# Order of the row stores, throwaway products on TensorE, and the order behind the experts in a hybrid decoder step

## Chip, cores and metric

One NeuronCore of a Trainium2 chip runs the whole program; the kernel is written by hand in Bass, with its own semaphores. The metric is the device time of one execution in microseconds. The kernel before took 856.63 us, the median of three runs (854.76 to 859.32).

## What is computed

A decoder layer over 520 rows of width 1024: 512 prompt rows and 8 sample rows. A mixer (gated short convolution beside four-head retention) is followed by a mixture of 32 experts and a gated embedding. Cut from the reference to what the change touches:

```python
h = h + mixer(rmsnorm(h, g_mix), ...)
x = rmsnorm(h, g_ffn)
# top-1 of 4 groups, then top-2 of its 8 experts; cw holds the two weights of a row
for e in range(32):
    hid = silu(x @ w_gate[e]) * (x @ w_up[e])       # width 512
    y = y + cw[:, e:e+1] * (hid @ w_down[e])
h = h + y
gate = sigmoid(rmsnorm(h, g_ple) @ w_ple_gate)      # 1024 x 1024
h = h + (p @ w_ple_proj) * gate                     # p: 256 columns
y_out = rmsnorm(h, g_final)
```

All weights are f32; those of the experts are 201 MB, and each expert is read once.

## The kernel before

**Head (0 to 277 us).** The rows lie transposed in SBUF. TensorE (PE) runs a list of jobs, `JOBS`; each writes one of four pairs of PSUM banks, and ScalarE (ACT) or VectorE (DVE) reads it. The last jobs are `wo` (output projection, eight column blocks), `tp` (transposing the new rows back, eight blocks), `lg` (router logits) and `ss` (sums of squares), then routing: DVE scales the logits by 1/rms (`route_logits`), picks group and experts (`route_choose`), and PE runs `rk` (ranks of each row in its expert, from `chosen`), `ix` and `iy` (the index tables of 64 places for each expert, from the masks of `hot_rows`) and `tot` (rows per expert). `ix` becomes `index`, which the gathers use.

**Rows in DRAM.** The experts gather their rows from `h_rows` in DRAM, half a row of 512 columns and 16 columns of 1/rms at a time. POOL (GpSimd) writes it: `store_rows` for each of the four entries of `STORES`, each one large store (prompt rows) and one small (sample rows). Before the last entry it waits for `rows_ready`, a copy that DVE makes between `route_logits` and `route_choose` (L1187), and issues four stores of 1/rms (L641, L642). Then it clears two tiles, waits for all twelve stores (`h_stored`) and for the index, and gathers (L655).

**Weights.** SyncE (SP) issues the weight loads in program order. A unit is 2 MB; an expert takes three. The ring has six slots; three units more, for expert 2, lie in spare space in pieces (`load_spare`, L465). SP loads what fits, waits for the first gather (`xg_loaded[0]`) before the last five pieces of the third spare unit, and then for each slot to come free: after the first expert's gate-and-up (`gu_done`) two loads (L526), and so on in turn (L538).

**Experts.** For each expert PE transposes the gathered rows (L1677), DVE copies them out (L1347), PE runs gate and up (L1698, two records a product), ACT the silu (L833), DVE the product (L1336), PE transposes (L1704) and runs down (L1713), ACT copies out (L837), and POOL scatters to `y_rows` (L661) and gathers for the expert two further on. POOL loads the final gain `g_fin_b` (L690) once, after the scatter of expert 3.

**Behind the experts.** `TAIL` is PE's list there: `pp` (projection of p, L1551 for a full tile and L1526 for the sample rows), `u` (transposes of a tile's rows, L1797), then gating: `pg` for the sample rows (f32 products, L1526), `pa` and `pb` for the two halves of a full tile (three products each of split high and low parts, L1821), `pc` for the last quarter. The tiles come in the order of `TAIL_TILES`: the eight sample rows first (turn 0), then the four prompt tiles. For each tile DVE sums the two experts' rows into h (`combine`, L1387), multiplies the transposed rows by the gain and forms their low part (`split_rows`, L1403 and L1413), ACT forms their high part (`high_rows`, L902), squares and root (`gate_root`, L910 and L912), and the sigmoid (`sigmoid`, L947); DVE multiplies and adds (`gated`, L1435 and L1436), ACT takes the final root (`final_root`, L919 and L921), DVE norms (`final_norm`, L1445), SP stores. The gate's weights are split into high and low parts in four portions (`gate_high_part`, `gate_low_part` L1462). Every engine runs its instructions in the order of the code, so what stands behind a wait waits too.

Of the kernel before, what the change touches and what calls it, by code (L numbers as in the profile page):

```python
# [98 lines left out]
TAIL = [("pp", _t) for _t in range(NT - 1)] + [("u", 0), ("pp", NT - 1), ("u", 1), ("pg", 0)]  # L99
# [47 lines left out]
HR = 528  # L147
STORES = [(0, 2), (2, 4), (4, 6), (6, KD)]


def build(nc, a, o):
# [8 lines left out]
    with ExitStack() as ctx:  # L160
# [210 lines left out]
        h_stored, lt_loaded, rows_ready = sem("h_stored"), sem("lt_loaded"), sem("rows_ready")  # L371
        pp_loaded = sem("pp_loaded")
# [61 lines left out]
        def _(sp):  # L434
# [79 lines left out]
            load_spare(0, 4)  # L514
            for n in range(4):
                load_spare(1, n)
            for n in range(3):
                load_spare(2, n)
            sp.wait_ge(xg_loaded[0], 16)
            for n in range(3, 8):  # L520
                load_spare(2, n)
# [69 lines left out]
        def _(pool):  # L591
# [43 lines left out]

            for c0, c1 in STORES[:-1]:
                store_rows(c0, c1)

            pool.wait_ge(rows_ready, 1)
            for half in range(2):  # L640
                pool.dma_start(h_full[:, :, half, 512:HR], rstd_rows[:, 0:4, :]).then_inc(h_stored, 16)  # L641
                pool.dma_start(h_few[:, half, 512:HR], rstd_rows[0:NB, 4, :]).then_inc(h_stored, 16)  # L642
            store_rows(*STORES[-1])
# [5 lines left out]
            pool.wait_ge(h_stored, 16 * (2 * len(STORES) + 4))  # L649
# [39 lines left out]
            pool.wait_ge(down_done, 3)  # L689
            pool.dma_start(g_fin_b, a["g_final"].to_broadcast([P, D])).then_inc(late_loaded, 16)  # L690
            with pool.Fori(2, NE // 2 - 1) as i:
                pair_of_experts(i, True)
            pair_of_experts(NE // 2 - 1, False)
            base = 2 * NE - 2
# [20 lines left out]
        def _(act):  # L715
# [45 lines left out]
            for n, (kind, c) in enumerate(JOBS):  # L761
# [60 lines left out]
                elif kind == "tp":  # L822
                    at = slice(c * P, (c + 1) * P)
                    nc.scalar.activation(xh[:, 0:4, at], b[:, 0:SEQ].rearrange("p (t c) -> p t c", t=4), ACT.Copy)
                    nc.scalar.activation(xh[0:NB, 4, at], b[0:NB, SEQ:SEQ + P], ACT.Copy).then_inc(act_jobs, 1)

# [66 lines left out]
            project(2)  # L893
            project(3)

            def high_rows(n):
                width = KD * TILES[TAIL_TILES[n]][1]
                act.wait_ge(u3_ready, n + 1)
                if n >= 2:

                    act.wait_ge(pe_tail, REST.pe(GATES[gates(n - 1) - 1]))
# [3 lines left out]
            def gate_root(n):  # L905
# [5 lines left out]
                                          accum_out=stats[0:m, 25 + t:26 + t]))  # L911
                nc.scalar.activation(stats[0:m, 30 + t:31 + t], stats[0:m, 25 + t:26 + t], ACT.Sqrt,  # L912
# [42 lines left out]
            high_rows(0)  # L955
            project(NT - 1)
            gate_root(0)
            for n in range(NT):
                if n + 1 < NT:

                    high_rows(n + 1)
                sigmoid("pa" if n else "pg", n)
                if n:
                    final_root(n - 1)
                if n + 1 < NT:
                    gate_root(n + 1)
                if n:
                    sigmoid("pb", n)
# [9 lines left out]
        def _(dve):  # L978
# [187 lines left out]
            for n, (kind, c) in enumerate(JOBS):  # L1166
# [9 lines left out]
                if kind == "ss":  # L1176
# [6 lines left out]
                    if c == 1:  # L1183
# [3 lines left out]
                        V.tensor_copy(rstd_rows, wide(stats[:, 10:15], [P, NT, HR - 512])).then_inc(rows_ready, 1)  # L1187
# [205 lines left out]
            def split_rows(n):  # L1393
# [5 lines left out]
                if n >= 2:  # L1399

                    dve.wait_ge(dve_tail, n - 1)
# [3 lines left out]
                                wide(col["gple"], [P, KD, m]), ALU.mult).then_inc(u3_ready, 1)  # L1405
                dve.wait_ge(u3_ready, n + 1)
                more = n + 1 < NT
                if n == 0:
                    gate_low_part(2)
                if more and n != 1:  # L1410
                    combine(n + 1, 0)
                dve.wait_ge(u3_hi_ready, n + 1)
                V.tensor_tensor(u3_lo[n % 2][:, 0:width], u3T[n % 2][:, 0:width], u3_hi[n % 2][:, 0:width],  # L1413
                                ALU.subtract).then_inc(dve_tail, 1)
                if n == 1:
                    gate_low_part(3)
                    combine(n + 1, 0)
                if more:
                    combine(n + 1, 1)
# [45 lines left out]
            dve.wait_ge(late_loaded, 16)  # L1465
# [5 lines left out]
            split_rows(0)  # L1471
            gate_rstd(0)
            for n in range(NT):
                if n + 1 < NT:
                    split_rows(n + 1)
                gated("pa" if n else "pg", n)
                if n:
                    final_norm(n - 1)
                if n + 1 < NT:
                    gate_rstd(n + 1)  # L1480
                if n:
                    gated("pb", n)
            dve.wait_ge(part_square, 2)
            link(V.tensor_tensor(stats[:, 45:46], stats[:, 42:43], stats[:, 43:44], ALU.add))
            V.tensor_scalar(stats[:, 45:46], stats[:, 45:46], 1.0 / D, EPS, ALU.mult, ALU.add).then_inc(part_sum, 1)
            gated("pc", NT - 1)
# [4 lines left out]
        def _(pe):  # L1491
# [38 lines left out]
            def spread(out, column, tile):  # L1530

                r0, m = TILES[tile]
                return mm(out[:, r0:r0 + m], column[0:m, :].to_broadcast([m, P]), ident[0:m, 0:m], start=True, stop=True)

# [24 lines left out]
            for n, (kind, c) in enumerate(JOBS):  # L1559
# [92 lines left out]
                elif kind == "rk":  # L1652

                    pe.wait_ge(lt_loaded, 16)
# [5 lines left out]
                elif kind == "ix":  # L1660

                    pe.wait_ge(hot_done, 1)
# [4 lines left out]
                elif kind == "tot":  # L1667
                    for s in range(NT):
                        last = mm(b[:, 0:NE], lt16[:, 1, :], chosen[:, s, :], start=(s == 0), stop=(s == NT - 1))
                last.then_inc(pe_jobs, 1)  # L1670
# [106 lines left out]
            for n, (kind, turn) in enumerate(TAIL):  # L1777
                b = pair(n)
                if n == 3:
# [18 lines left out]
                else:  # L1798

                    pe.wait_ge(u3_hi_ready, turn + 1)  # L1800
                    pe.wait_ge(dve_tail, turn + 1)
# [128 lines left out]
```

## Time and profile before

| | |
|---|---|
| median of three runs | 856.63 us |
| profiled execution | 857.87 us, its span 856.0 us |
| busy share of the span | PE 84%, PE weight loads 51%, DVE 33%, ACT 21%, POOL 12% |
| mean granted TensorE clock | 0.979 of 2.4 GHz |
| DMA | 257.18 MB, mean 300 GB/s |
| chain that ended last | PE 47%, DMA 39% (38% the experts' weights), DVE 3% |

Times in the profile count from the start of the span. The chain is followed back from the last instruction: at each step to what released it. The granted clock is 1.00 at 2.4 GHz and 0.50 at 1.2 GHz. A line number is that of the code above; where a helper is used the line is the helper's. The share of DMA is the mean busy share of 16 DMA engines.

### The profile page before, as it was taken

To read this page: it belongs to the slowest core of one execution; us is meant where nothing else is said; L and a number is where in the kernel's file an instruction comes from. 1 tells how busy PE (TensorE), PEld (TensorE's weight loads), DVE (VectorE), ACT (ScalarE), POOL (GpSimd) and SP (SyncE) were. 2 spreads that over 40 slices of the span, in tenths; PEclk is the share of its full clock that TensorE was granted. 3 is DMA by queue.
4 is the path that set the end of the run, shared out by engine and by line. 5 is a ranking of instruction groups with operands and counts; after the bars stand their busy time and mean duration, and the time that the engine had idled before them with its cause. 6 is when DMAs were issued, how large, how long until landed. Compare 5 with 4: busy or idle time off the path is not lost.

```text
span 856.0 us, 11000 instructions
## 1 busy us (share of the span) xinstructions
PE 719.6 (84%) x4330; PEld 440.3 (51%) x4330; DVE 279.8 (33%) x500; ACT 182.3 (21%) x276; POOL 104.2 (12%) x163
## 2 busy tenths in 40 slices
PE   8999999999999389888777777777777777778995
PEld 8998899989998134332222222222222222223685
DVE  5564578575433621110100101101001001015774
ACT  7243312223323100100000000000000000006666
POOL 0500000000010312112111121121111111100000
PEclk9999999999999599999999999999999999999898
DMA  9542116542935878999999999999999999993201
GB/s 350 214 173 68 58 62 253 208 160 74 361 122 184 295 295 335 374 426 426 425 427 426 427 428 424 428 426 427 426 428 425 428 425 427 427 415 142 99 27 74
DMA packets 33297, 257.18 MB, mean 300 GB/s; under 512 B 6644, under 2 KB 7204, under 8 KB 19560
## 3 DMA queue, kind: packets, MB, share of 16 engines
q1 hardware_dynamic: 25232, 237.17, 67.3%
q0 software_dynamic: 7024, 18.07, 5.6%
q10 hardware_dynamic: 1008, 1.48, 0.5%
q8 instruction: 24, 0.39, 0.2%
q14 instruction: 9, 0.07, 0.0%
HBM read 249.96 MB, written 15.13 MB: 310 GB/s over the span
## 4 chain that ended last, share of the span: by engine, by line
PE 47%; DMA 39%; DVE 3%; issue 2%; ACT 1%; SPq 1%; POOL 0%; DVEq 0%; POOLq 0%
DMA arena<-in_w_exp 38%; PE ps L1518 19%; PE ps L1698 12%; PE ps L1821 4%; PE ps L1713 3%; PE ps L1551 2%; PE ps L1627 1%; PE ps L1650 1%; DMA h_rows<-xh 1%; PE ps L1617 1%; SPq L538 1%; PE ps L1526 1%; PE ps L1797 1%; DVE region_u L1336 0%; ACT region_u L833 0%
## 5 line engine op out<-in xcount | busy, mean ns | idle before, releaser
L1698 PE MATMUL ps<-arena,region_u 128*64 128x512 f32 x992 | 227.6, 603 | 58.1 <-DMA arena<-in_w_exp 57.1
L1698 PEld LDWEIGHTS ps<-arena,region_u 128*64 128x64 f32 x992 | 70.3, 138 | 213.8 <-issue 139.4
L1336 DVE SCALAR_TENSOR_TENSOR region_u<-ps,small,region_u 128x256 f32<-128x256 f32 x32 | 15.5, 484 | 392.3 <-ACT region_u L833 392.3
L1518 PE MATMUL ps<-u_hi,w_hi 128*128 128x260 f32 x448 | 129.3, 289 | 4.4 <-issue 2.3
L1518 PE MATMUL ps<-u_lo,w_hi 128*128 128x260 f32 x448 | 126.6, 283 | 0.0
L1518 PE MATMUL ps<-u_hi,w_low 128*128 128x260 f32 x448 | 126.4, 282 | 0.0
L1713 PE MATMUL ps<-arena,region_u 128*64 128x512 f32 x496 | 113.3, 598 | 7.7 <-DMA arena<-in_w_exp 3.7
L1518 PEld LDWEIGHTS ps<-u_hi,w_hi 128*128 128x128 f32 x448 | 84.4, 188 | 6.3 <-issue 4.0
L1518 PEld LDWEIGHTS ps<-u_lo,w_hi 128*128 128x128 f32 x448 | 84.3, 188 | 0.2
L1518 PEld LDWEIGHTS ps<-u_hi,w_low 128*128 128x128 f32 x448 | 84.4, 188 | 0.0
L661 POOL DMA_INDIRECT y_rows<-region_v,scol x32 | 33.3, 1041 | 377.6 <-ACT region_v L837 377.6
L833 ACT ACTIVATE region_u<-ps,small 128x256 f32<-128x256 f32 x32 | 15.2, 473 | 278.5 <-PE ps L1698 278.5
L1713 PEld LDWEIGHTS ps<-arena,region_u 128*64 128x64 f32 x496 | 34.9, 136 | 66.1 <-issue 58.7
L837 ACT ACTIVATE region_v<-ps 128x512 f32<-128x512 f32 x32 | 19.1, 597 | 173.8 <-PE ps L1713 173.8
L1114 DVE TENSOR_TENSOR w_low<-arena,w_hi 128x1024 fp32r<-128x1024 f32 x35 | 43.0, 1232 | 20.9 <-ACT w_hi L735 20.7
L1704 PE MATMUL ps<-ident,region_u 128*128 128x128 f32 x64 | 14.0, 300 | 35.1 <-DVE region_u L1336 35.1
L735 ACT ACTIVATE w_hi<-arena 128x1024 fp32r<-128x1024 f32 x35 | 36.7, 1048 | 12.8 <-PE ps L1518 12.7
L1704 PEld LDWEIGHTS ps<-ident,region_u 128*128 128x128 f32 x64 | 6.4, 140 | 63.3 <-DVE region_u L1336 63.3
L1518 PE MATMUL ps<-mix_lo,w_hi 128*128 128x260 f32 x128 | 36.7, 287 | 0.0
L655 POOL DMA_INDIRECT region_u<-h_rows,gcol x30 | 31.3, 1043 | 25.9 <-POOL gcol L676 25.9
L1821 PE MATMUL ps<-gate_hi,u_hi 128*128 128x512 f32 (+1 forms) x72 | 26.7, 371 | 0.0
L1821 PE MATMUL ps<-gate_lo,u_hi 128*128 128x512 f32 (+1 forms) x72 | 26.4, 366 | 0.0
(275 smaller groups left out, 814.8 us busy)
## 6 DMA issues: line engine op xcount, KB each, us to landing
arena<-in_w_exp SPq DMA_DIRECT2D x91, 2048.0 KB, 25.8
arena<-in_w_in SPq DMA_DIRECT2D x35, 512.0 KB, 3.5
arena<-in_w_exp SPq DMA_DIRECT2D x8, 512.0 KB, 3.9
arena<-in_w_ple_gate SPq DMA_DIRECT2D x2, 2048.0 KB, 23.6
region_q<-in_w_exp SPq DMA_DIRECT2D x12, 256.0 KB, 13.0
region_u<-in_xt SPq DMA_DIRECT2D x2, 1040.0 KB, 6.1
arena<-in_state_ret POOLq DMA_DIRECT2D x2, 1024.0 KB, 8.2
xh<-v_few POOLq DMA_DIRECT2D x1, 2048.0 KB, 9.1
```

The source lines that it names most:

```text
L655: pool.indirect_dma_start(out=xg[b], out_offset=None, in_=h_rows, in_offset=bass.IndirectOffsetOnAxis(ap=at, axis=0), bounds_check=2 * T - ...
L661: pool.indirect_dma_start(out=y_half, out_offset=bass.IndirectOffsetOnAxis(ap=scol[:, b:b + 1], axis=0), in_=out_sb[b], in_offset=None, bo ...
L735: nc.scalar.activation(w_hi[n % WIN_HIGH], w_raw[:, n % WIN_SLOTS, :], ACT.Copy).then_inc(w_hi_ready, 1)
L837: nc.scalar.activation(out_sb[b], ps[:, 6 + b, :], ACT.Copy).then_inc(out_sem, 1)
L1114: V.tensor_tensor(w_low[:, n % WIN_SLOTS, :], w_raw[:, n % WIN_SLOTS, :], w_hi[n % WIN_HIGH], ALU.subtract).then_inc(w_lo_ready, 1)
L1336: V.scalar_tensor_tensor(hs[b], ps[:, 2 + b, 256:512], rs[b], sg[b], ALU.mult, ALU.mult).then_inc(out_sem, 1)
L1518: last = mm(halves(out)[:, half, :], w[:, k, :], u[:, cols], start=(k == 0 and s == 0), stop=(k == KD - 1 and s == 2))
L1551: last = mm(b[0:m, half * 512:half * 512 + 512], pT[:, k, r0:r0 + m], w[:, k, half * 512:half * 512 + 512], start=(k == 0), stop=(k == 1))
L1698: last = mm(ps[side * 64:side * 64 + 64, 2 + b, :], xv[:, k // 4, k % 4, :], rows(k % 4 * 2 + side), start=(k == 0), stop=(k == KD - 1))
L1704: last = tr(ps[:, 4 + b, k * P:(k + 1) * P], hs[b][:, k * P:(k + 1) * P], ident[:, :])
L1713: last = mm(ps[side * 64:side * 64 + 64, 6 + b, :], hv, rows(q * 2 + side), start=(q == 0), stop=(q == 3))
L1821: last = mm(b[:, cols], u[:, k, :], w, start=(k == 0 and i == 0), stop=(k == KD - 1 and i == 2))
```

## The change

It has two places. At the start of the experts: the four row stores are issued one after the other; the copy of 1/rms is made on ACT, and ACT issues its four stores, counted on a semaphore of their own, `rstd_stored`, for which the gathers wait as well. SP waits for the eight row stores before it issues the spare loads of the second unit, and for the first gather before all eight pieces of the third. PE runs 28, 8 and 16 products of the identity with itself (`spin`, results never read): ahead of the waits of `rk` and of `ix`, and behind `tot`. The load of `g_fin_b` stands behind the last expert's scatter.

Behind the experts: the projection of the sample rows comes ahead of that of the last full tile. DVE sums two tiles ahead of the first transposes. `split_rows` becomes `gained` and `low_rows`; the sample rows, whose gating is f32, get no high and low parts. `gate_root` becomes `gate_square` and `gate_sqrt`, and the roots of the first two turns stand together. The sample rows' sigmoid, multiplication and final root stand behind tile 1's preparation on ACT and DVE. The last `gated` stands ahead of the wait for two squares.

```diff
-TAIL = [("pp", _t) for _t in range(NT - 1)] + [("u", 0), ("pp", NT - 1), ("u", 1), ("pg", 0)]
+TAIL = [("pp", 0), ("pp", 1), ("pp", 2), ("pp", NT - 1), ("pp", 3), ("u", 0), ("u", 1), ("pg", 0)]
...
+SPIN = (28, 8, 16)
...
             load_spare(0, 4)
+
+            sp.wait_ge(h_stored, 16 * 2 * len(STORES))
             for n in range(4):
                 load_spare(1, n)
-            for n in range(3):
-                load_spare(2, n)
             sp.wait_ge(xg_loaded[0], 16)
-            for n in range(3, 8):
+            for n in range(8):
                 load_spare(2, n)
...
-            for c0, c1 in STORES[:-1]:
+            for c0, c1 in STORES:
                 store_rows(c0, c1)
-
-            pool.wait_ge(rows_ready, 1)
-            for half in range(2):
-                pool.dma_start(h_full[:, :, half, 512:HR], rstd_rows[:, 0:4, :]).then_inc(h_stored, 16)
-                pool.dma_start(h_few[:, half, 512:HR], rstd_rows[0:NB, 4, :]).then_inc(h_stored, 16)
-            store_rows(*STORES[-1])
...
-            pool.wait_ge(h_stored, 16 * (2 * len(STORES) + 4))
+            pool.wait_ge(h_stored, 16 * 2 * len(STORES))
+            pool.wait_ge(rstd_stored, 16 * 4)
             pool.wait_ge(index_done, 1)
...
-            pool.wait_ge(down_done, 3)
-            pool.dma_start(g_fin_b, a["g_final"].to_broadcast([P, D])).then_inc(late_loaded, 16)
             with pool.Fori(2, NE // 2 - 1) as i:
                 pair_of_experts(i, True)
             pair_of_experts(NE // 2 - 1, False)
+            pool.dma_start(g_fin_b, a["g_final"].to_broadcast([P, D])).then_inc(late_loaded, 16)
...
+            act.wait_ge(rstd_done, 2)
+            act.wait_ge(pe_jobs, HEAD.pe(("wo", KD - 1)))
+            nc.scalar.activation(rstd_rows, stats[:, 10:15].unsqueeze(2).to_broadcast([P, NT, HR - 512]),
+                                 ACT.Copy).then_inc(rows_ready, 1)
+            act.wait_ge(rows_ready, 1)
+            for half in range(2):
+                act.dma_start(h_full[:, :, half, 512:HR], rstd_rows[:, 0:4, :]).then_inc(rstd_stored, 16)
+                act.dma_start(h_few[:, half, 512:HR], rstd_rows[0:NB, 4, :]).then_inc(rstd_stored, 16)
...
             project(2)
+            project(NT - 1)
             project(3)
...
-            high_rows(0)
-            project(NT - 1)
-            gate_root(0)
-            for n in range(NT):
+            high_rows(1)
+            gate_square(0)
+            gate_sqrt(0)
+            gate_square(1)
+            gate_sqrt(1)
+            sigmoid("pg", 0)
+            for n in range(1, NT):
                 if n + 1 < NT:
-
                     high_rows(n + 1)
-                sigmoid("pa" if n else "pg", n)
-                if n:
-                    final_root(n - 1)
+                sigmoid("pa", n)
+                final_root(n - 1)
                 if n + 1 < NT:
-                    gate_root(n + 1)
-                if n:
-                    sigmoid("pb", n)
+                    gate_square(n + 1)
+                    gate_sqrt(n + 1)
+                sigmoid("pb", n)
...
-                        V.tensor_copy(rstd_rows, wide(stats[:, 10:15], [P, NT, HR - 512])).then_inc(rows_ready, 1)
...
             combine(0, 0)
             combine(0, 1)
-            split_rows(0)
+            combine(1, 0)
+            combine(1, 1)
+            gained(0)
+            gained(1)
+            low_rows(1)
+            gate_low_part(2)
             gate_rstd(0)
-            for n in range(NT):
+            combine(2, 0)
+            combine(2, 1)
+            gate_rstd(1)
+            gate_low_part(3)
+            dve.wait_ge(late_loaded, 16)
+            for n in range(1, NT):
                 if n + 1 < NT:
-                    split_rows(n + 1)
-                gated("pa" if n else "pg", n)
-                if n:
-                    final_norm(n - 1)
+                    gained(n + 1)
+                    if n + 2 < NT:
+                        combine(n + 2, 0)
+                    low_rows(n + 1)
+                    if n + 2 < NT:
+                        combine(n + 2, 1)
+                if n == 1:
+                    gated("pg", 0)
+                gated("pa", n)
+                final_norm(n - 1)
                 if n + 1 < NT:
                     gate_rstd(n + 1)
-                if n:
                     gated("pb", n)
+            gated("pb", NT - 1)
+            gated("pc", NT - 1)
             dve.wait_ge(part_square, 2)
...
-            gated("pc", NT - 1)
             last_norm()
...
+            def spin(out, count):
+
+                for _ in range(count):
+                    mm(out[:, 0:P], ident[:, :], ident[:, :], start=True, stop=True)
...
                 elif kind == "rk":
 
+                    spin(b, SPIN[0])
                     pe.wait_ge(lt_loaded, 16)
...
                 elif kind == "ix":
 
+                    spin(b, SPIN[1])
                     pe.wait_ge(hot_done, 1)
...
+                    spin(pair(n + 1), SPIN[2])
                 last.then_inc(pe_jobs, 1)
...
-                if n == 3:
+                if n % 4 == 3:
                     pe.wait_ge(out_ready, NE)
...
-                    pe.wait_ge(u3_hi_ready, turn + 1)
-                    pe.wait_ge(dve_tail, turn + 1)
+                    pe.wait_ge(u3_ready, turn + 1)
+                    if turn:
+                        pe.wait_ge(u3_hi_ready, turn)
+                        pe.wait_ge(dve_tail, turn)
```

## Rows read from the trace of the kernel before

**Rows 1.** Windows, 100 us: busy us of each engine, granted clock, DMA share, GB/s.
```profile
400.00:500.00 100.00, 75.90 (x348) 25.67 (x348) 9.96 (x24) 6.42 (x12) 17.27 (x28) 1.00 1.01 427
```

**Rows 2.** The chain that ended last, 277 to 318 us: start, us, what.
```profile
277.73 0.77 POOL h_rows L641
...
281.06 7.18 DMA h_rows<-xh
...
289.17 3.25 DMA region_u<-h_rows,index
292.55 1.10 PE ps L1677 x4
...
294.58 10.02 PE ps L1698 x32
...
310.36 6.89 PE ps L1698 x32
```

**Rows 3.** Timeline of DVE, routing and end: start, us, operation, what released it.
```profile
277.20 0.24 DVE L1187 COPY region_m<-stats 128x80 f32<-128x80 f32 x1
...
286.77 0.25 DVE L1323 TENSOR_SCALAR index<-ps,small 128x32 int32<-128x32 f32 x1 [1.02 <-PE ps L1540]
...
850.16 0.43 DVE L1435 TENSOR_TENSOR region_q<-region_q,region_u 128x256 f32<-128x256 f32 x1
```

**Rows 4.** Windows of 1 us, columns as in rows 1.
```profile
280.00:281.00 1.00, 0.00 (x0) 0.00 (x0) 0.86 (x5) 0.00 (x0) 1.00 (x2) 0.50 0.73 229
...
303.00:304.00 1.00, 1.00 (x8) 0.28 (x4) 0.00 (x0) 0.00 (x0) 0.00 (x0) 1.00 0.00 0
...
792.00:793.00 1.00, 0.00 (x0) 0.00 (x0) 0.98 (x2) 0.92 (x2) 0.00 (x0) 0.50 0.00 0
```

**Rows 5.** The chain that ended last, behind the experts.
```profile
773.19 13.93 PE ps L1551 x32
...
793.09 1.94 PE ps L1797 x8
795.03 5.45 PE ps L1526 x64
800.48 5.71 PE ps L1821 x24
```

**Rows 6.** The page's DMA issues: count, KB each, median us to landing.
```profile
h_rows<-xh POOLq DMA_DIRECT2D x4, 8.0 KB, 4.2
h_rows<-region_m POOLq DMA_DIRECT2D x2, 32.0 KB, 5.7
...
region_q<-in_g_final POOLq DMA_DIRECT2D x1, 512.0 KB, 13.6
region_m<-y_rows SPq DMA_DIRECT2D x2, 1024.0 KB, 4.7
```

**Rows 7.** Timeline of PE in routing.
```profile
282.68 0.56 PE L1658 MATMUL ps<-region_m,meanw 128*128 128x32 f16 x15 [5.97 <-DVE region_m L1023]
285.70 1.30 PE L1540 MATMUL ps<-region_m 128*64 128x32 f16 x30 [2.47 <-DVE region_m L1039]
```

**Rows 8.** The chain that ended last, one retention job of four f32 products.
```profile
67.08 0.89 PE ps L1633 x8
```

**Rows 9.** Timeline of PE, the program's first products.
```profile
1.35 6.03 PE L1557 MATMUL ps<-region_z 128*128 128x128 f32 x28 [1.35 <-DVE region_z L1147]
```

**Rows 10.** Groups by line, 780 to 856 us: count, busy us, mean ns, idle before.
```profile
L1387 DVE SCALAR_TENSOR_TENSOR xh<-region_v,wk,xh 128x1024 f32<-128x1024 f32 x4 | 5.1, 1280 | 0.1
...
L1403 DVE TENSOR_TENSOR region_u<-ps,small 128x1024 f32<-128x1024 f32 x4 | 4.9, 1222 | 3.2 <-PE ps L1797 3.2
...
L910 ACT ACTIVATE region_u<-xh 128x1024 f32<-128x1024 f32 x4 | 4.2, 1043 | 0.0
```

**Rows 11.** Timeline of ACT, tile 1's first sigmoid.
```profile
809.68 1.28 ACT L947 ACT_TABLE_LOAD   x1
810.98 0.69 ACT L947 ACTIVATE region_u<-ps,stats 128x512 f32<-128x512 f32 x1
```

More of the change, by code:

```diff
@@ L371, in build @@
         h_stored, lt_loaded, rows_ready = sem("h_stored"), sem("lt_loaded"), sem("rows_ready")
+        rstd_stored = sem("rstd_stored")
         pp_loaded = sem("pp_loaded")
@@ L898, in high_rows @@
                 act.wait_ge(u3_ready, n + 1)
-                if n >= 2:
+                if n >= 3:
                     act.wait_ge(pe_tail, REST.pe(GATES[gates(n - 1) - 1]))
@@ L903, in high_rows, with gate_square @@
                                      ACT.Copy).then_inc(u3_hi_ready, 1)
-            def gate_root(n):
+            def gate_square(n):
                 t = TAIL_TILES[n]
@@ L911, in gate_root, with gate_sqrt @@
                                           accum_out=stats[0:m, 25 + t:26 + t]))
+            def gate_sqrt(n):
+                t = TAIL_TILES[n]
+                m = TILES[t][1]
                 nc.scalar.activation(stats[0:m, 30 + t:31 + t], stats[0:m, 25 + t:26 + t], ACT.Sqrt,
@@ L1391, in combine, with gained @@
                     link(ins)
-            def split_rows(n):
+            def gained(n):
                 b = pair(REST.at[("u", n)])
@@ L1399, in split_rows @@
                 if n >= 2:
-                    dve.wait_ge(dve_tail, n - 1)
                     dve.wait_ge(pe_tail, REST.pe(GATES[gates(n - 1) - 1]))
@@ L1405, in split_rows, with low_rows @@
                                 wide(col["gple"], [P, KD, m]), ALU.mult).then_inc(u3_ready, 1)
+            def low_rows(n):
                 dve.wait_ge(u3_ready, n + 1)
[L1407 to L1419, printed above, removed]
+                dve.wait_ge(u3_hi_ready, n)
+                V.tensor_tensor(u3_lo[n % 2], u3T[n % 2], u3_hi[n % 2], ALU.subtract).then_inc(dve_tail, 1)
             def gate_rstd(n):
@@ L1463, in gate_low_part @@
                                 ALU.subtract).then_inc(gate_lo_ready, 1)
-            dve.wait_ge(late_loaded, 16)
             dve.wait_ge(down_done, NE - 1)
```

## Prediction

> **What bounds the kernel now.** I read the windows first. From 400 to 500 us the DMA engines are busy all the time (share 1.01, 427 GB/s) while PE computes 75.9 of 100 us: the experts are paced by their weights [rows 1]. So in the long middle nothing counts but the moment from which the weight stream is never short of a free buffer, and how many bytes it carries. I then read the chain of waits around the start of the experts [rows 2]: PE's work ends at 276.7 us, the last small row store is issued at 281.06 and lands 7.18 us later (288.24), the first gather is issued at 289.17 and lands after 3.25, four transposes take 1.10 and the first expert's 32 gate-and-up records 10.02, where the next expert's take 6.89. Then the timelines: the indices are ready at 286.77 + 0.25 = 287.02 [rows 3], so the gather waits 1.2 us for the row store, not for routing. The windows of 1 us say why the first expert is slow: PE stopped at 276.7 and the granted clock is at 0.50 (1.2 of 2.4 GHz) from 280 until 300.7 [rows 4]. They also show the DMA engines at 0.00 in 303 to 304 [rows 4]: all free buffers are full at 298.5 and the stream waits for the first expert's products (304.6). It is short of buffers once more (337 to 344) until expert 3's gate-and-up products end at 343.1, and never after. Expert 0 to 3 run at PE's pace, so an earlier end of the first gate-and-up moves the whole stream.
>
> Last I read the chain behind the experts [rows 5]: four projected tiles on PE (13.93 us from 773.19), then a gap: PE waits for the sums of the first full tile on DVE, its clock falls to 0.50 [rows 4], eight transposes take 1.94 and the sample rows' gating 5.45, and the first gate products start at 800.48. From there PE is never idle until the last gate products (847.3).
>
> **The change, part by part.** The sum is made against the profiled execution, 857.87 us (span 856.0, 1.87 around it), which is 1.24 above the median of the three runs, 856.63.
>
> *Gather.* POOL loses four issues of the 1/rms columns (277.73 to 280.29), so the last row store is issued at 278.6 in place of 281.06. SP now holds 2 MB and 0.75 MB of spare weights until the row stores have landed; the small store then meets only the end of an earlier load and takes its median 4.2 [rows 6]: landed at 282.8 (loaded as before, 7.2: 285.8). The 1/rms stores go to ACT's queue behind its last copy (277.8); at POOL's issue price, 0.77 and 0.53 [rows 2], the last is out by 280.7, and with the 5.7 they had [rows 6] they land by 286.4. The index chain becomes the last: DVE drops one copy of 0.24, 0.16 of it in the chain [rows 3]; the 20 index products ran at half clock, 0.87 of the 1.30 us of 30 records [rows 7], and take half of it at full clock: -0.44. Index ready 287.02 - 0.16 - 0.44 = 286.4; with the 0.93 that the gather needed after its release (288.24 to 289.17) it starts at 287.3: **-1.8**. It meets the end of the held weights (2 MB from 283 at 427 GB/s: until 288), as it met the end of the old ones: landing 3.25 stays.
>
> *Throwaway products.* Four f32 products of this size, each two records, took 0.89 us at L1633, 0.223 each [rows 8]. The program's first 14 took 6.03 us, 0.43 each, as if at the lower level [rows 9]. I take 0.223, because PE comes straight from busy work. 28 of them run from 276.7 to 282.9; the ranks could start at about 282.5 (before 282.68 [rows 7]), and DVE can't use them before 283.5, so the overhang of 0.4 is covered by DVE's own choice products. 8 end at 285.1, before the row masks at 285.4. 16 behind the totals run from 286.8 to 290.4; the gather lands at 290.6. PE has then no gap over 1 us, where its clock fell after 3.3 us idle. Transposes 0.60 in place of 1.10: **-0.5**. Gate and up 6.89 in place of 10.02 [rows 2]: **-3.1**. First gate-and-up ends at 299.2, not 304.6.
>
> *Held spare weights.* The 8 pieces of the third spare unit follow the first gather: from 290.6, 2 MB at 427 GB/s, in by 296. The first expert needs none of them and expert 2 starts near 318: cost 0, covered by DMA's idle stretch 298.5 to 305 [rows 4]. Without that cover it would be 2.75 MB / 427 = 6.4 us.
>
> *g_final.* Its 512 KB broadcast is issued at 351.4, inside the full stream (13.6 us to land [rows 6]), and moves behind the last scatter: 0.5 MB / 427 = **-1.2** (0 at least, if it rode in gaps). There it is needed only at the first final norm, over 20 us later; it can cost the next loads 1.2.
>
> Head: -1.8 - 0.5 - 3.1 - 1.2 = **-6.6**, all carried by the stream to the end of the experts.
>
> *First gate products* (times as before's, unshifted). PE: 773.19 + 13.93 + 1.05 for the sample projection, now ahead of tile 3 = 788.2; transposes of the sample rows 0.6 and of tile 0 at full clock 0.9 to 1.0: 789.9. The two tiles' sums fill DVE's wait: 781.7 to 784.3 and, with the second load landing 4.7 after its issue at 779.9 [rows 6], 784.6 to 787.2. Then DVE 1.22, ACT 1.06, DVE 1.23 with their gaps: the split rows are ready at 793.6. Beside it the sample gating at full clock: between 3.4 (5.45 with its 3.6 us at half clock counted half) and 4.2 (four times 1.05): 793.3 to 794.1. First gate products 793.7 for 800.48 [rows 5]: **-6.7** (-6.0 to -7.1).
>
> *What is late next.* The sample rows' gating and final root now stand behind tile 1's on DVE and ACT. With the durations of [rows 10, 11]: DVE is free at 801.2 (the fourth low part 2.3 us behind two sums); gain 1.22, sum 1.28, low 1.23, sum 1.28, sample gating 2.43: 808.7. ACT's square for the final norm waits for that: 1.23, table 1.28, root 0.29, the next tile's square 1.23 and root 0.29, table 1.28, sigmoid 0.68: 815.0; DVE gating 1.38, gain 1.22, sum 1.28, low 1.23: 820.1. PE needs it after 793.7 + 5.7 + 0.9 + 10.9 + 0.9 + 5.5 = 817.6: **+2.5** (0 to 4). DVE and ACT have 10.8 us of work and waits a tile against PE's 11.8, so it isn't repeated.
>
> *Edits at no cost.* The sample rows' high and low parts go (0.25 on ACT, 0.22 on DVE, neither read by a product); the order of the projections only moves 1.05 us of PE, counted above; the wait of PE for the last expert's output on two more jobs is long met.
>
> *End.* The last gating products no longer wait for two squares: they ran at 850.16 [rows 3] though their sigmoid ended at 847.8. The chain then is table, root, two squares on ACT, sum, root: **-1.1**.
>
> Tail: -6.7 + 2.5 - 1.1 = -5.3. Sum: -11.9; 857.87 - 11.9 = 846.0 for an execution like the profiled one, and with its 1.24 above the median, 844.7.
>
> **The rivals.**
> A. *The clock still falls* (a gap in front of the first expert or too little work in the products). For it: at the program's start such products ran at the lower rate, and the index products didn't bring it back. Against: no gap nears 3.3 us. It returns 3.1 + 0.5 + 0.4: **848.7**.
> B. *The ACT-DVE round paces the last tiles.* The chain under "what is late next" is all waits of ACT and DVE for each other; it holds two switches of table. Were a switch twice as dear as the 1.30 between the start of a load (809.68) and that of the sigmoid behind it (810.98) [rows 11], PE's stall would be 5.1: **847.3**. Against: that row.
> The Trainium skill ("ScalarE: Activation LUTs", What ACT_TABLE_LOAD costs) has such a rule: each switch costs a drain of about 1.38 us besides the 1.28 of the load. The trace disagrees, as the sigmoid starts right behind the load; by the page the stall would be 5.3 and the time 847.5.
> C. *The stream doesn't move*: the held 2.75 MB are paid after all and the gain of the first expert is eaten by filling. For: 6.4 us is about the idle 6.5. Against: they are in by 296, before 299.2. Only g_final's 1.2 and the tail remain: **850.1**.
> D. *Slower*: the throwaway products at 0.43 us. The 28 hold PE until 288.8, ranks and masks follow, 8 more hold the index by 1.1: index at 294.3; 16 more hold the transposes until 301.4; at half clock the first gate-and-up ends near 313.5, 8.9 later instead of 5.4 earlier: 844.7 + 14.3 = **859.0**. It turns the gain into a loss from about 0.38 us a product. Against: PE is at the upper level when they begin.
>
> **How the numbers follow.** Forecast 0.70, A 0.08, B 0.10, C 0.08, D 0.04. The forecast's own range is 841 to 848: no stall in the tail (-2.5), stall 4 (+1.5), g_final 0 (+1.2), the runs' own spread. For 8 in 10 it must reach A and B and most of C: **840.5 to 851.5**. A measurement can tell about 0.5% (4.3 us) from no change: faster than 852.3 holds the forecast, A, B and nearly all of C; D lies within 0.5% or a little above. Faster 0.90, same 0.07, slower 0.03.
>
> **What would show it.** Granted clock 1.00 from 276 to 320; the 28 products in 6.2 us; the gather issued at 287 to 288, released by the index; first gate-and-up in 6.9 us, ending near 299; expert 3's near 338; the last expert weights near 757; then gate products starting 20.5 us (before 27.3) after the first projection, a PE gap of 2 to 3 us before the third tile's gate products, and 1 us less behind the last. A clock of 0.50 near 290 (A, D), DMA busy without a gap between 290 and 300 (C) or a larger PE gap (B) would show me wrong.

## The result and the profile after

The changed kernel takes 848.53 us, the median of five executions (847.68 to 849.6), beside 856.63 for the kernel before (five, 854.76 to 859.32): a ratio of 0.990 (95% interval 0.9874 to 0.9925). So it is faster, by 8.1 us where 11.9 was forecast, and the time lies in the range. The profiled execution has a span of 845.9 us (before 856.0) and a mean clock of 0.993 (before 0.979).

I cut both traces at the same six events: DVE's 1/rms reciprocal at the end of the head (276.01 us before, 273.58 after), the start of the first expert's silu (304.62, 302.17), the last expert's last gate-and-up records (763.83, 759.81), the end of its down products (773.18, 769.16), the first gate products (800.48, 789.83) and the start of the last norm (852.14, 841.97).

| stretch | before | after | difference | predicted |
|---|---|---|---|---|
| start to 1/rms | 276.01 | 273.58 | -2.4 | 0 |
| 1/rms to first silu | 28.61 | 28.59 | 0.0 | -5.4 |
| first silu to last gate-and-up | 459.21 | 457.64 | -1.6 | -1.2 |
| last gate-and-up to last down | 9.35 | 9.35 | 0 | 0 |
| last down to first gate products | 27.30 | 20.67 | -6.6 | -6.7 |
| first gate products to last norm | 51.66 | 52.14 | +0.5 | +1.4 (+2.5 - 1.1) |

The first row isn't put down to the change: ahead of that reciprocal only SP's spare loads differ (from 273.39 us on in the kernel before, held in the changed one), and in the ten profiled executions of this study it starts anywhere from 273.58 to 276.82. The latest of them is that of experiment 7, which has the changed kernel's head. The other rows add up to -7.7, near the 8.1 of the medians. The tail came nearly as worked out (-6.1 for -5.3), and the forecast's 5.4 us between routing and the first expert didn't come at all.

The chain that ended last, after, around the start of the experts and behind them (start, us, what):
```profile
285.14 5.22 DMA region_u<-h_rows,index
290.50 0.64 PE ps L1700 x4
...
292.07 10.08 PE ps L1721 x32
302.17 0.48 ACT region_u L837
...
769.16 10.50 PE ps L1571 x24
779.66 0.98 PE ps L1541 x16
780.64 3.63 PE ps L1571 x8
784.27 1.63 PE ps L1820 x16
...
789.83 4.58 PE ps L1846 x19
...
815.12 5.73 PE ps L1846 x24
...
841.97 0.75 DVE xh L1455
```
Beside [rows 2] the gather takes 5.22 us in place of 3.25, and the first gate-and-up (now L1721) is no faster: 10.08 for 10.02. Behind the experts the gap of [rows 5] has gone, and the transposes (L1820) run straight behind the projections.

The timeline of PE in routing (start, us, line, operation, count, idle before and its releaser):
```profile
274.13 6.42 PE L1553 MATMUL ps<-ident 128*128 128x128 f32 x56
280.38 0.53 PE L1679 MATMUL ps<-region_m,meanw 128*128 128x32 f16 x15
280.76 2.03 PE L1553 MATMUL ps<-ident 128*128 128x128 f32 x16
283.08 0.86 PE L1560 MATMUL ps<-region_m 128*64 128x32 f16 x30 [0.29 <-DVE region_m L1049]
283.87 0.29 PE L1691 MATMUL ps<-region_m,meanw 128*128 128x32 f16 x5
284.01 3.82 PE L1553 MATMUL ps<-ident 128*128 128x128 f32 x32
290.50 0.63 PE L1700 MATMUL ps<-ident,region_u 128*128 128x128 f32 x4 [2.67 <-DMA region_u<-h_rows,index]
292.07 10.05 PE L1721 MATMUL ps<-arena,region_u 128*64 128x512 f32 x32 [0.94 <-DVE region_u L1356]
```
The throwaway products (L1553) take 6.42 us for 28, 0.229 each, as taken from [rows 8]. The index products take 0.86 for the 1.30 of [rows 7], the transposes of the gathered rows 0.63: all at full clock. But the last throwaway product ends at 287.83, and the gather lands at 290.36. PE idles for 2.67 us and, after 0.63 of transposes, for 0.94 more. Windows of 1 us (busy us of PE, PE loads, DVE, ACT, POOL; granted clock, DMA share, GB/s):
```profile
282.00:283.00 1.00, 0.79 (x8) 0.60 (x6) 0.96 (x3) 0.00 (x0) 0.00 (x0) 1.00 0.00 0
...
286.00:287.00 1.00, 1.00 (x12) 1.00 (x11) 0.83 (x6) 0.00 (x0) 0.70 (x2) 1.00 1.03 363
...
290.00:291.00 1.00, 0.50 (x4) 0.42 (x4) 0.00 (x0) 0.00 (x0) 0.00 (x0) 1.00 0.03 9
291.00:292.00 1.00, 0.12 (x2) 0.00 (x0) 0.74 (x3) 0.00 (x0) 0.00 (x0) 0.63 0.54 119
292.00:293.00 1.00, 0.93 (x4) 0.32 (x6) 0.86 (x5) 0.00 (x0) 0.18 (x1) 0.50 1.00 348
```
The clock, which in [rows 4] was at 0.50 from 280 on, holds until 291 and falls just as the first expert begins: rival A, by a gap that I hadn't seen. The DMA share says where the gap comes from. It is 0.00 at 282 to 283, and about 1 while the gather is under way (issued 285.14): the held 2 MB of spare weights, issued from 282.26 on, ride beside it. The timelines of POOL (the last small row store) and of SP's queue (the first held piece):
```profile
276.41 0.53 POOL L636 DMA_DIRECT2D h_rows<-xh  x1
...
282.26 0.33 SPq L467 DMA_DIRECT2D region_v<-in_w_exp  x1
```
The store lands 5.8 us after its issue, and with it the weights are released.

At the end the last products are followed by the last norm 9.30 us later (832.67 to 841.97, before 841.55 to 852.14: 10.59).

### The profile page after: what moved, and what is told of

Same layout as the page of the kernel before. It is cut to its first block, busy times and chain, and to the rows that moved or that the text cites. A ratio compares the mean times of both kernels' runs of the same rounds, so it can differ in the third digit from the quotient of the medians.

```text
span 845.9 us, 11206 instructions
## 1 busy us (share of the span) xinstructions
PE 725.5 (86%) x4434; PEld 447.7 (53%) x4434; DVE 278.9 (33%) x498; ACT 179.5 (21%) x274; POOL 100.8 (12%) x159
## 4 chain that ended last, share of the span: by engine, by line
PE 45%; DMA 38%; DVE 5%; ACT 2%; issue 2%; SPq 1%; DVEq 0%; POOLq 0%; ACTq 0%
DMA arena<-in_w_exp 38%; PE ps L1533 19%; PE ps L1721 12%; PE ps L1736 3%; PE ps L1846 3%; PE ps L1571 2%; PE ps L1647 1%; PE ps L1670 1%; PE ps L1637 1%; SPq L540 1%; DMA region_u<-h_rows,index 1%; DVE region_u L1345 0%; ACT region_u L837 0%; PE ps L1608 0%; DVE xh L1396 0%
## 5 line engine op out<-in xcount | busy, mean ns | idle before, releaser
L1721 PE MATMUL ps<-arena,region_u 128*64 128x512 f32 x992 | 227.6, 603 | 56.7 <-DMA arena<-in_w_exp 55.7
L1721 PEld LDWEIGHTS ps<-arena,region_u 128*64 128x64 f32 x992 | 70.4, 138 | 212.0 <-issue 140.0
L652 POOL DMA_INDIRECT region_u<-h_rows,gcol x30 | 31.3, 1042 | 26.0 <-POOL gcol L673 24.8
```

The lines of the kernel that those rows point to most:

```text
L652: pool.indirect_dma_start(out=xg[b], out_offset=None, in_=h_rows, in_offset=bass.IndirectOffsetOnAxis(ap=at, axis=0), bounds_check=2 * T - ...
L1721: last = mm(ps[side * 64:side * 64 + 64, 2 + b, :], xv[:, k // 4, k % 4, :], rows(k % 4 * 2 + side), start=(k == 0), stop=(k == KD - 1))
```

## The experiments

My theory after the result: the head's gain was lost because the held weights lengthen the gather by 2 us, this opens the gap on PE, and the clock falls in it (3 us more). The rivals: the throwaway products are useless or harmful in themselves; the order of the stores does the work; the price is in the weight stream, not at its start. The kernel before took 857.08 us beside experiments 1 to 4 and 855.76 beside 5 to 8; so across the two groups the ratios are compared, not the microseconds. The stage that the first four expectations name, from the end of PE's last transposes of the head to the end of the first gate-and-up, is 27.9 us before and after.

**1. Ten more throwaway products behind the totals.** Only the gap on PE is filled; the gather isn't touched.
```diff
-SPIN = (28, 8, 16)
+SPIN = (28, 8, 26)
```


> The changed kernel with 26 throwaway products behind the totals in place of 16. Stage measured: from the end of TensorE's last transposes of the head to the end of the first expert's gate-and-up; it is 27.9 us in the kernel before and in the changed one. Theory (the clock falls because PE is idle for 2.7 us before the late gather lands): ten more products at 0.24 us keep PE busy until about 290.2, the granted clock stays 1.00, the first gate-and-up takes 6.9 in place of 10.05, the stage is about 24.8 and the whole 3 us shorter (845.5). Rival (products of this size don't hold the clock in front of the expert, or something else lowers it): gate-and-up stays at 10, stage 27.9, whole 848.5.


Measured: 846.58 us, ratio 0.9875 (0.985 to 0.9899). PE's timeline:
```profile
274.97 7.43 PE L1553 MATMUL ps<-ident 128*128 128x128 f32 x56
...
285.71 6.05 PE L1553 MATMUL ps<-ident 128*128 128x128 f32 x52
292.07 0.63 PE L1700 MATMUL ps<-ident,region_u 128*128 128x128 f32 x4 [0.31 <-DMA region_u<-h_rows,index]
293.64 7.09 PE L1721 MATMUL ps<-arena,region_u 128*64 128x512 f32 x32 [0.94 <-DVE region_u L1356]
```
The gap is 0.31 and the first gate-and-up takes 7.09: the filled gap gives the 3 us, which the times alone don't separate from the changed kernel. The stage is 25.6, nearer the theory's 24.8 than the rival's 27.9. The stretch from 1/rms to the first silu is 26.99, only 1.6 less than after, because the first 28 products took 7.43 and not 6.42. In this execution the clock dipped for a few us around 275 (0.87 in 270 to 275, 0.79 in 275 to 280), and the throwaway products, which stand ahead of the ranks, pass such a dip on: the gather was issued 13.05 us after 1/rms, for 11.56. Without such products ahead of them (experiment 3) the ranks start 6.5 us after 1/rms, here 8.4.

**2. The gather first.** SP waits for the first gather before all the spare loads; PE's products stay as they are.
```diff
-            sp.wait_ge(h_stored, 16 * 2 * len(STORES))
+            sp.wait_ge(xg_loaded[0], 16)
             for n in range(4):
                 load_spare(1, n)
-            sp.wait_ge(xg_loaded[0], 16)
             for n in range(8):
```


> The changed kernel, but SP waits for the first gather ahead of all spare weights of the second and third unit (4 MB behind the gather, none ahead of it). Theory (the held 2 MB, released by the row stores at 282.3, share the DMA engines with the gather and make it land after 5.2 in place of 3.25 us): gather lands in 3.3 us or less, PE idles under 1 us, the clock stays 1.00, gate-and-up 6.9, stage 22.8 to 23; stream short of buffers until then as before, so the whole is 5 us shorter (843.5). Rival (the gather is slow because of the 1/rms columns' small packets or the DMA's own start): gather 5.2, stage 27.9, whole 848.5. If 4 MB behind the gather don't land in time, expert 2 waits and part is given back.


Measured: 844.61 us, ratio 0.9849 (0.9823 to 0.9875). The chain:
```profile
287.24 3.30 DMA region_u<-h_rows,index
```
PE's timeline:
```profile
286.11 3.82 PE L1552 MATMUL ps<-ident 128*128 128x128 f32 x32
290.68 0.63 PE L1699 MATMUL ps<-ident,region_u 128*128 128x128 f32 x4 [0.75 <-DMA region_u<-h_rows,index]
292.25 7.09 PE L1720 MATMUL ps<-arena,region_u 128*64 128x512 f32 x32 [0.94 <-DVE region_u L1355]
```
With idle DMA engines the gather lands in 3.30; the 16 products that were there all along reach to within 0.75 us of it, the clock stays at 1.00, and gate-and-up takes 7.09. From 1/rms to the first silu: 23.70, 4.9 us less than after, and nothing of it is lost later (first silu to last gate-and-up 457.52, last down to last norm 72.78). That is the forecast's head within half a us (28.61 - 5.4 = 23.2). The stage is 23.0, as the theory had it. All 4 MB of the second and third spare unit, now issued from 290.56 on, cost nothing in the stream.

**3. No throwaway products.**
```diff
-SPIN = (28, 8, 16)
+SPIN = (0, 0, 0)
```


> The changed kernel without any throwaway product. Theory (they only speed the index products and the first transposes, since the clock falls anyway before the first gate-and-up): clock 0.50 from about 3.3 us behind the last transposes, the index 0.45 later, the transposes 0.45 longer, gate-and-up 10.0 as now: stage 28.8, whole 0.9 us longer (849.4). Rival (they hold the routing back or cost DMA or power elsewhere): whole same or shorter.


Measured: 850.91 us, ratio 0.9928 (0.9907 to 0.9948). PE's timeline:
```profile
283.62 1.30 PE L1560 MATMUL ps<-region_m 128*64 128x32 f16 x30 [2.46 <-DVE region_m L1049]
...
291.46 1.08 PE L1700 MATMUL ps<-ident,region_u 128*128 128x128 f32 x4 [6.29 <-DMA region_u<-h_rows,index]
293.49 9.93 PE L1721 MATMUL ps<-arena,region_u 128*64 128x512 f32 x32 [0.94 <-DVE region_u L1356]
```
As in [rows 2, 7] everything runs at the lower level, and gate-and-up is as slow as after. From 1/rms to the first silu 29.40: the products as changed are worth 0.8 us (0.4 in the indices, 0.46 in the transposes), not the 3.6 to 4 that they were made for. The stage is 28.7 for the theory's 28.8. The medians put the products at 2.4 (850.91 - 848.53), with intervals that overlap.

**4. No hold.** The spare loads are issued as in the kernel before (four and three pieces ahead of the first gather, five behind it), and the rest of the change stays.
```diff
-            sp.wait_ge(h_stored, 16 * 2 * len(STORES))
             for n in range(4):
                 load_spare(1, n)
+            for n in range(3):
+                load_spare(2, n)
             sp.wait_ge(xg_loaded[0], 16)
-            for n in range(8):
+            for n in range(3, 8):
```


> The changed kernel with the spare weights issued as in the kernel before (2.75 MB ahead of the wait for the gather, nothing held for the row stores). Theory (holding them buys an earlier end of the row stores and pays it back in the gather): the row stores land about 2.5 us later (285.8 on the changed kernel's axis less the shift, near 283.5), still about when the index is ready; the gather meets a DMA that is nearly done and lands in 3.3 to 4 us, PE idles under 2 us and the clock may hold: stage 23 to 26, whole 2 to 5 us shorter. Rival (the hold is what makes the gather start early): gather issued 2 us later, stage 27.9 or more.


Measured: 853.71 us, ratio 0.996 (0.9936 to 0.9984). The chain:
```profile
278.78 12.97 DMA h_rows<-region_m
...
292.77 3.43 DMA region_u<-h_rows,index
296.34 1.10 PE ps L1701 x4
...
298.36 9.79 PE ps L1722 x32
```
The stage is 32.2 us, where my theory had 23 to 26: it missed, and the rival (the hold is what makes the gather start early) came out, by more than it said. The small 1/rms stores, issued on ACT's queue, take 12.97 us to land beside the weight loads, where POOL's took 5.7 [rows 6]. They hold the gather 6 us longer (17.53 us from 1/rms, after 11.56); the gather itself then lands in 3.43, since the loads are done. From 1/rms to the first silu 32.94, 4.35 more than after. So the hold is needed as soon as ACT stores the columns, and it pays for itself; only its end was in the wrong place.

**5. The final gain back in the stream.**
```diff
+            pool.wait_ge(down_done, 3)
+            pool.dma_start(g_fin_b, a["g_final"].to_broadcast([P, D])).then_inc(late_loaded, 16)
             with pool.Fori(2, NE // 2 - 1) as i:
                 pair_of_experts(i, True)
             pair_of_experts(NE // 2 - 1, False)
-            pool.dma_start(g_fin_b, a["g_final"].to_broadcast([P, D])).then_inc(late_loaded, 16)
```


> The changed kernel with the 512 KB load of the final gain back where it was, inside the weight stream. Stage measured: from the first silu to the last expert's second half of gate-and-up (459.2 us in the kernel before, 457.6 in the changed one). Theory (a full stream pays for every byte, 512 KB at 427 GB/s = 1.2 us): stage 458.8 to 459.2, whole 1.2 to 1.6 us longer (849.9). Rival (the 1.6 us come from elsewhere, the load was free): stage 457.6, whole 848.5.


Measured: 849.91 us, ratio 0.9916 (0.989 to 0.9942), 1.4 above the changed kernel, which alone the intervals don't separate. The trace does: first silu to last gate-and-up is 459.32, as before (459.21), where every kernel with the load behind the experts has 457.50 to 457.80. The term is 1.7 us.

**6. The sample rows' gating one sum earlier on DVE.** It should take the stall ahead of the third tile's gate products.
```diff
                     low_rows(n + 1)
+                    if n == 1:
+                        gated("pg", 0)
                     if n + 2 < NT:
                         combine(n + 2, 1)
-                if n == 1:
-                    gated("pg", 0)
                 gated("pa", n)
```


> The changed kernel with the sample rows' multiplication and sum on DVE ahead of the second sum of the tile two further on (1.28 us earlier). Stage measured: from the end of the last expert's down products to the last norm (78.95 us before, 72.8 changed). Theory (PE's gap of 1.5 us before the third tile's second gate products is set by the chain sample gating, final square and roots, sigmoid, gating, gain, low part): everything in it starts 1.28 earlier, the gap falls to about 0.2, stage 71.5, whole 1.3 us shorter. Rival (the table switches and ACT's own work pace it): gap stays 1.5, stage 72.8.


Measured: 848.07 us, ratio 0.9901 (0.9873 to 0.993), against 0.9899 the same within the intervals. The group of PE behind the experts that waits for DVE (busy us, mean ns, idle before and its releaser), first in the profile after:
```profile
L1846 PE MATMUL ps<-gate_hi,u_hi 128*128 128x512 f32 x56 | 22.3, 398 | 1.8 <-DVE u_lo L1419 1.8
```
And in this one:
```profile
L1846 PE MATMUL ps<-gate_hi,u_hi 128*128 128x512 f32 x56 | 22.2, 397 | 0.6 <-DVE u_lo L1419 0.6
```
PE's idle time behind DVE's low part falls by 1.2, and the stretch from the last down to the last norm from 72.81 to 71.58. So it works where it should, by an amount that only the trace can tell.

**7. The head's half of the change alone**, the tail as before.
```diff
-TAIL = [("pp", 0), ("pp", 1), ("pp", 2), ("pp", NT - 1), ("pp", 3), ("u", 0), ("u", 1), ("pg", 0)]
+TAIL = [("pp", _t) for _t in range(NT - 1)] + [("u", 0), ("pp", NT - 1), ("u", 1), ("pg", 0)]
```
(and the code of `split_rows`, `gate_root` and the tail loops of ACT, DVE and PE as in the kernel before)


> The kernel before with only the first half of the change (row stores, 1/rms on ACT, held weights, throwaway products, final gain behind the experts), and the order behind the experts as before. Theory (that half gives nothing until the first silu and 1.6 us in the stream; the rest of the gain is behind the experts): from DVE's 1/rms to the first silu 28.6 as in both, stream stage 457.6, stage behind the experts 78.9, whole 1.6 us shorter than before (855). Rival (the halves depend on each other, as the final gain lands beside the first sums): behind the experts longer than 78.9.


Measured: 854.28 us, ratio 0.9978 (0.9961 to 0.9995). So the head as changed is worth 0.2%, and the tail the rest of the 1.0%. Its chain, at the first expert and behind the last:
```profile
288.35 5.17 DMA region_u<-h_rows,index
293.65 0.64 PE ps L1688 x4
...
295.22 8.58 PE ps L1709 x32
...
773.21 4.60 DMA region_q<-in_g_final
```
The gather is as slow as after, 5.17, and PE idles for 2.6 us again. This time the clock dipped only for 3 to 4 us (0.50 in 295 to 298) and the first gate-and-up took 8.58, so that 1/rms to the first silu is 27.01 and not the 28.6 expected: the same gap cost 1.5 us here and 3 in the profile of after. Behind the experts it takes 79.21, 0.25 more than before: in the old order DVE waits for the final gain ahead of all its work there, and with its load (4.60 us) moved behind the experts DVE starts 7.1 us after the last down products, for 3.4 before. So the rival of the expectation is right, by a quarter of a us.

**8. Experiments 2 and 6 together.**


> The changed kernel with all spare weights behind the first gather and the sample rows' gating ahead of the second sum. Theory (the two gains lie in different stages and add): first silu 23.7 us after DVE's 1/rms as in the run with the gather first, behind the experts 71.5, whole 843.3, 14 us shorter than before. Rival (the second gain is hidden): 844.6.


Measured: 843.34 us, ratio 0.9854 (0.9829 to 0.9879), the lowest median of all. But its ratio is no better than that of experiment 2 (0.9849), whose kernel before was slower too: that the two gains add is seen in the stretches of the trace, not in the times. The chain:
```profile
286.73 3.17 DMA region_u<-h_rows,index
290.04 0.64 PE ps L1699 x4
...
291.61 7.11 PE ps L1720 x32
...
786.45 4.58 PE ps L1845 x19
...
810.54 5.73 PE ps L1845 x24
```
The gather is short, gate-and-up at full clock, and from the last down to the last norm 71.60 us pass, as in experiment 6. The dip at 270 to 280 was there too (0.91, 0.75), so 1/rms to the first silu took 25.05 and not the 23.7 expected.

The stretches of all kernels, in us, from the one profiled execution of each:

| kernel | 1/rms to silu | of it to the gather's issue | gather | gate-and-up | silu to last gate-and-up | last down to last norm |
|---|---|---|---|---|---|---|
| before | 28.61 | 13.16 | 3.25 | 10.02 | 459.21 | 78.96 |
| after | 28.59 | 11.56 | 5.22 | 10.08 | 457.64 | 72.81 |
| 1 more products | 26.99 | 13.05 | 5.09 | 7.11 | 457.56 | 72.77 |
| 2 gather first | 23.70 | 11.56 | 3.30 | 7.11 | 457.52 | 72.78 |
| 3 no products | 29.40 | 11.96 | 5.31 | 9.95 | 457.69 | 72.80 |
| 4 no hold | 32.94 | 17.53 | 3.43 | 9.79 | 457.56 | 72.80 |
| 5 gain in stream | 29.04 | 11.55 | 5.63 | 10.12 | 459.32 | 72.81 |
| 6 sample first | 28.70 | 13.05 | 5.12 | 8.81 | 457.80 | 71.58 |
| 7 head alone | 27.01 | 11.53 | 5.17 | 8.58 | 457.50 | 79.21 |
| 8 both | 25.05 | 13.04 | 3.17 | 7.11 | 457.69 | 71.60 |

## Why the prediction was right in sign and short in size

- **Gather, -1.8**: its issue came 1.6 us nearer to 1/rms (11.56 for 13.16), released by the indices and no longer by the row stores, and the indices were 0.5 earlier. Right. Of what moved the row stores only the hold was taken out by itself (experiment 4); the order of the stores and ACT's part were not taken apart.
- **"Landing 3.25 stays"**: the step that failed. I put the end of the held weights at 288, 0.7 us behind the gather's start, and took the old landing because the gather before had met the end of a load as well. Two terms of that time were mis-sized. The last row store took 5.8 us to land for the 4.2 that I took, so the weights left 8.7 us after 1/rms (282.26 - 273.58) where the plan had 6.8 to 7 (282.8 to 283, less 276.01). And they kept the engines busy for 7.7 us, until about 290, for the planned 5; the gather was issued only 2.9 us after them, for the planned 4.3, and so had nearly 5 us of load beside it instead of 0.7. It took 5.22, in five more kernels 5.09 to 5.63. With the engines idle it takes 3.17 to 3.43 (experiments 2, 4 and 8). The term is +2.0. The old 3.25 was that of a gather whose load ended about 1 us behind its issue: in the trace of before the DMA share (last but one) falls there.
```profile
289.00:290.00 1.00, 0.00 (x0) 0.00 (x0) 0.83 (x6) 0.00 (x0) 0.83 (x1) 0.50 1.04 402
290.00:291.00 1.00, 0.00 (x0) 0.00 (x0) 0.67 (x4) 0.00 (x0) 0.69 (x2) 0.50 0.47 148
```
- **Gate and up at full clock, -3.1**: came out 0, as its condition failed. I had written that PE has no gap over 1 us; it has one of 2.67 and, behind 0.63 us of transposes, one of 0.94. I set only the first kind against the 3.3 us of idleness of before, and left the second out. (The clock of before came back at 300.5 and not at 300.7, as I had read it; nothing hangs on that.) Gaps of 0.31, 0.75 or 0.62 with the same 0.94 behind them keep the clock (experiments 1, 2 and 8). Filling the gap, or taking away its cause, brings the 3 us back, so the mechanism is shown. Its size varies: 1.5 to 1.7 us in experiments 6 and 7 (gaps of 2.57 and 2.62), about 3 after (2.67) and in experiment 5 (3.08).
- **Transposes, -0.5**: 0.64 for 1.10. Right.
- **Held weights, 0**: right for the stream (457.5 to 457.8 whether they start at 282 or 290.6), wrong as an account of the hold, since its price was paid by the gather.
- **The final gain, -1.2**: -1.6 between the two traces, 1.7 in experiment 5. The bytes count in full, and a little more.
- **First gate products, -6.7**: -6.6. The sample gating took 3.64, at the lower of my two bounds, which is 3.65 and not the 3.4 that I wrote (5.45 with 3.6 of it halved); the products (789.83) waited 0.36 us for the low part.
- **The stall, +2.5**: PE idled 1.46 us ahead of the third tile's products, and the rest of the stretch is 0.3 longer than before: +1.8. The links came as worked out, ACT's table loads among them; the round of ACT and DVE was only about 1 us shorter than my sum.

ACT's timeline in that stretch:
```profile
807.96 1.28 ACT L956 ACT_TABLE_LOAD   x1
809.25 0.69 ACT L956 ACTIVATE region_u<-ps,stats 128x512 f32<-128x512 f32 x1
```
The sigmoid starts 1.29 us after the load does (1.30 in [rows 11]). Rival B, with its stall of 5.1, fell. By the Trainium skill ("ScalarE: Activation LUTs", What ACT_TABLE_LOAD costs) a drain of about 1.38 us comes on top of each load; the trace again shows none, as those 1.29 us leave no room for it.

- **End, -1.1**: 10.59 to 9.30, -1.3. Right.

**The rivals.** A is what happened in its main term, the slow first gate-and-up (3.1), and by the first of its two causes, a gap in front of the first expert. Its other two terms did not come, as the indices and transposes kept their 0.4 and 0.5, and the slower landing (2.0) is not in it. So the agreement in the number, 848.7 worked out and 848.53 measured, is chance. I gave it 0.08 because I priced the gap from one landing time; a row for the landing beside a running load was at hand, in the row stores' 7.18 us [rows 2], and would have made A likelier. In the traces the head falls short by 5.4 (landing 2.0, gate-and-up 3.2, issue 0.2), while the final gain gives 0.4 more than forecast and the tail 0.8. C fell in its reason: the held weights cost the stream nothing (457.6 for 459.2), although the first expert's gain was gone, as it says. D fell too, though a dip of the clock shows a small piece of it: 28 products in 7.4 us hold the ranks by 1.0 and more.

Open: why the clock dips in the head while PE is busy with the same instructions: at 245 to 255 in the profiles of before and of experiments 2 and 7 (0.66 to 0.73 in 250 to 255; 1/rms at 275.68 to 276.82), at 270 to 280 in those of 1, 6 and 8, and not in those of after, 3, 4 and 5 (1/rms at 273.58, 274.06, 275.24 and 273.58, so that it isn't the only cause of the spread). In experiments 1, 6 and 8 the gather is issued 1.5 us later, as much as a term of the forecast; what the earlier dip costs wasn't told apart from the rest of the spread. Why ACT's small stores were so slow in experiment 4 was not taken apart either. Their place in time is hardly it: they were issued 2.0 to 3.5 us after 1/rms, POOL's in the kernel before 1.7 to 3.8. The queue and the last large row store, which now runs beside them, are left.

## What to carry over

Hold a bulk load until the small transfer that the chain waits for has landed, not until the step ahead of it has, when the stream has slack later: here the same 2 MB cost nothing behind the gather and 5 us beside it. Work that only keeps PE's clock up must reach to the very end of the wait, so size it from the longest landing seen under load, and put none of it ahead of a chain of short steps where a dip of the clock would be passed on. A gap that is only a little shorter than one that cost the clock elsewhere (here 2.7 us beside 3.3) can't be taken as harmless, above all with a second one close behind it. And where one transfer is meant to be over before another starts, price the release and the length of the first from what it meets: here both were too short, by 1.6 and 2.7 us.

## What the runs showed that I had not expected

- The same gather takes 3.17 to 3.43 us with idle DMA engines (three traces) and 5.09 to 5.63 beside 2 MB of weights (six), with no value in between.
- The last of four small stores of 1/rms on ACT's queue took 12.97 us to land beside the weight loads; POOL's had taken 5.7 [rows 6]. With no load issued behind them, all twelve stores were in by 282.3, 5 us after the last issue.
- With nearly the same gap on PE (2.57 to 2.67 us, and 0.94 more) the granted clock fell at 291.3 after, at 294.9 in experiments 6 and 7, and came back between 298 and 299 in all three: a later fall cost less.
- 0.5 MB of another load inside a full weight stream cost 1.7 us, not the 1.2 that its bytes make at 427 GB/s.
